# Attention with a top-k search on ScalarE: the counts of each tile's search begin one step later

## What is computed

```python
logits = jnp.einsum('bqhd,bsd->bqhs', iqb, ik)
index = jnp.einsum('bqh,bqhs->bqs', iwb, jax.nn.relu(logits)) * idx_scale
index = jnp.where(causal[None], index.astype(jnp.float32), -jnp.inf)
_, sel = lax.top_k(index, topk)          # topk = 256
kg = jax.vmap(lambda kb, ib: kb[ib])(k, sel)
s = jnp.einsum('bqhd,bqkd->bqhk', qb, kg) * scale
```

## Time and profile before

| | us |
|---|---|
| time before, median of 3 runs (lowest to highest) | 3646.22 (3642.06 to 3647.02) |
| the profiled execution's own time | 3653.36 |
| its span, first to last instruction | 3651.6 |
| PE / DVE / ACT / POOL busy in it | 3431.7 / 2358.1 / 1804.7 / 1210.2 |
| first and last count (L1762) | 507.2 to 1955.0 |

### The profile page before, as it was taken

How to read it: one execution, slowest core, us unless ns; L and a number is a source line. 1 busy time by engine, 2 the same in 40 slices (tenths; PEclk the granted TensorE clock), 3 DMA queues, 4 the chain that set the end, 5 groups by cost and what they waited for, 6 DMA issues and landing times. The chain is left out here.

```text
span 3651.6 us, 55407 instructions
## 1 busy us (share of the span) xinstructions
PE 3431.7 (94%) x18952; PEld 2939.0 (80%) x18952; DVE 2358.1 (65%) x4874; ACT 1804.7 (49%) x3062; POOL 1210.2 (33%) x1966
## 2 busy tenths in 40 slices
PE   6999789899999999999999899799999999999998
PEld 6999767678888878888878688688888788888876
DVE  8999366677776677676674344865554657565354
ACT  3443346677777667867856333433323333333232
POOL 5243244454433333332222033532211425332031
PEclk9999899999999999999999999899999999999999
DMA  4345310000000000000000256232224542332444
GB/s 162 121 152 166 80 32 18 22 20 18 17 14 11 17 10 14 11 8 11 4 7 30 90 161 195 82 115 93 81 93 168 185 133 93 104 102 80 142 141 170
DMA packets 189762, 289.59 MB, mean 79 GB/s; under 512 B 33458, under 2 KB 129842, under 8 KB 189490
## 3 DMA queue, kind: packets, MB, share of 16 engines
q1 hardware_dynamic: 187412, 285.64, 23.8%
q10 hardware_dynamic: 2080, 0.52, 0.1%
HBM read 211.15 MB, written 74.97 MB: 78 GB/s over the span
## 5 line engine op out<-in xcount | busy, mean ns | idle before, releaser
L1755 ACT ACTIVATE shared<-a_ps_st 128x512 f32<-128x512 f32 x716 | 437.6, 615 | 289.8 <-PE a_ps_st L1641 147.4
L2866 PE MATMUL f_ps<-f_x_four,f_w_hi 128*128 128x512 f32 x1408 | 438.2, 393 | 11.4 <-DVE f_w_lo L3004 11.4
L2866 PE MATMUL f_ps<-f_x_three,f_w_hi 128*128 128x512 f32 x1056 | 325.5, 389 | 1.5 <-DVE f_w_lo L3004 1.5
L2866 PEld LDWEIGHTS f_ps<-f_x_four,f_w_hi 128*128 128x128 f32 x1408 | 266.6, 190 | 68.4 <-DVE f_w_lo L3004 13.0
L1665 PEld LDWEIGHTS a_ps_o<-a_vsl,shared 128*128 128x128 f32 x2176 | 297.7, 201 | 19.6 <-DVE a_fin L1972 0.7
L1463 POOL TENSOR_SCALAR a_tk<-a_tk,a_halves 128x1 f32<-128x1 f32 x336 | 108.7, 324 | 588.0 <-ACT a_junk_a L1762 586.3
L1665 PEld LDWEIGHTS a_ps_o<-a_dv,shared 128*128 128x128 f32 x2176 | 285.8, 194 | 12.3
L1665 PE MATMUL a_ps_o<-a_vsl,shared 128*128 128x65 f32 x2176 | 288.9, 278 | 0.0
L1665 PE MATMUL a_ps_o<-a_dv,shared 128*128 128x65 f32 x2176 | 276.7, 271 | 0.0
L2866 PE MATMUL f_ps<-f_x_four,f_w_lo 128*128 128x512 f32 x704 | 275.8, 392 | 0.0
L2899 PE MATMUL f_ps<-f_w_hi 128*128 128x512 f32 x680 | 265.6, 391 | 4.8 <-DVE f_w_lo L3013 4.8
(11 more groups left out here) (382 smaller groups left out, 8794.8 us busy)
## 6 DMA issues: line engine op xcount, KB each, us to landing
shared<-in_w_down SPq DMA_DIRECT2D x88, 512.0 KB, 3.4
px_raw<-in_x_t SPq DMA_DIRECT2D x48, 512.0 KB, 4.7
shared<-in_w_gate SPq DMA_DIRECT2D x44, 512.0 KB, 5.1
shared<-in_w_up SPq DMA_DIRECT2D x44, 512.0 KB, 4.8
g_scratch<-shared SPq DMA_DIRECT2D x22, 1024.0 KB, 7.5
shared<-g_scratch SPq DMA_DIRECT2D x88, 256.0 KB, 3.4
z_scratch<-p_z SPq DMA_DIRECT2D x16, 768.0 KB, 5.2
o_scratch<-a_oacc SPq DMA_DIRECT2D x32, 256.0 KB, 2.1
```

What stands on the lines that cost most here:

```text
L1755: act.activation(p_t[:, s % PT_RING, :], ps_st[s % ST_BANKS][:, :], ACT.Exp, scale=SCALE).then_inc(exp_done, 1)
L2866: mm = pe.matmul(out[:, :], w[:, j, k * P:(k + 1) * P], x_part(j, x)[:, k], start=(k == 0 and i == 0), stop=(k == 3 and i == 2))
```

## The change

One line in `Schedule.set_search`: the first step of the range over which a search's 24 counts are spread is begin + nch + 1 and no longer begin + nch. The last step, the number of counts and everything else of the plan are as they were.

```diff
@@ -833,7 +833,7 @@
                 self.chores[end + 3 + nch + c].append(("pick", t, c))
             self.chores[begin + nch].append(("set", t, 0))
             self.chores[end + 1 + nch].append(("room", t, 0))
-            a, b = begin + nch, end
+            a, b = begin + nch + 1, end
             for m in range(NSTEP):
                 self.counts[a + m * (b - a) // NSTEP].append((t, m))
             begin = end + 1
```

## The result

The change makes the kernel slower by a little: 3651.91 us (median of 17 runs, 3648.68 to 3660.65) against 3646.82 us for the kernel before on the same chips (17 runs, 3642.06 to 3648.86). The ratio is 1.0016, with a 95% interval of 1.0009 to 1.0022: 5 us lost, where 17 were forecast as gained. The profiled execution of the kernel after took 3651.62 us, its span is 3649.8. That is shorter than the span of 3651.6 in which the rows of before stand, though the medians say the opposite. That execution of before was 7 us over its median; a second trace of the kernel before stands further down beside it.

What follows compares the result with a forecast made beforehand. PE, busy 94% of the span, was taken as the bound, so only less idle time or a higher clock could pay. 8.0 + 7.5 - 1.5 - 2 + 5.1 = 17.1 us off 3646.2 gave 3629 us, range 3617 to 3643.

Steps and rivals of the forecast that it cites:

- (a): PE gaps ended by the late exponential at the sets of searches 7, 9, 10, 11, 14: 8.0 us saved.
- (b): PE gaps ended by an ACT copy behind a count, searches 4 to 7: 7.5 us saved.
- (c): Search 8: the first count's threshold move falls behind a POOL addition, so PE loses 1.5 us.
- (d): Other counts meet or leave POOL's waits for DVE's `a_fin`: 2 us lost, bounds 2 gained to 9 lost.
- (e): PE's clock after the gaps of searches 9, 10, 11, 14: 5.1 us gained, bounds 0 and 10.2.
- (f): Searches 2, 3, 12, 13 and 15 costed at nothing; DVE ends PE's stops at the sets of 12, 13, 15.
- The second: Rival: moved counts get behind POOL's additions in searches 2, 5, 8, 9; slower, 3657 us, chance 0.06.
- deciding point: ACT's waiting for POOL grows from 72.2 us by more than PE's saved idle, some 15 us.
- The sign that the prediction set for being wrong: ACT's wait for POOL grows as much as its wait for DVE falls, or PE's gaps stay, ended by DVE.
- The first rival: PE stops at the next bank DVE has not emptied, giving gains back within ten steps; 3642 us, chance 0.19.
- The third: Rival: DVE's set comes later by what ACT comes earlier, so ACT's wait stays; 3646 us, chance 0.02.

Runs made afterwards that it cites:

- two-step kernel: Against the kernel before, counts of searches 4 and 7 begin one step later, those of 9, 10, 11, 14 and 15 two: 3635.66 us, ratio 0.9972.
- All but the first: Count 0 of every search at its old step, the other counts as in the changed kernel; against the kernel before: 3652.91 us, ratio 1.0023.
- first alone: Only count 0 of searches 9 to 15 one step later than in the kernel before: 3644.28 us, ratio 0.9999.
- late alone: The change for searches 9 to 15 only, against the kernel before: 3642.67 us against 3645.02, ratio 0.9997.
- early alone: The change for searches 2 to 8 only, against the kernel before: 3658.04 us, ratio 1.0037.
- 6 alone: The change for search 6 only, against the kernel before: 3656.52 us against 3648.6, ratio 1.0011.

## Why the prediction was wrong

(a) held. The five gaps at the sets went from 1.28, 2.56, 3.07, 3.57 and 2.14 to 0.20, 1.07, 1.60, 2.14 and 0.26 us. That is 7.4 us; 8.0 was the sum. DVE is next, as it said, and the two-step kernel confirms it.

(b) held at most of the gaps it named and failed as a gain. Search 4's 7.05 us became 4.49 (2.6 saved, 2.1 forecast), search 5's gap of 1.15 and search 6's of 1.71 went, search 7's of 1.99 is 0.3; only search 5's second, 1.23, is still 1.06. That is 7.3 us; 7.5 was the sum. But the counts that moved away from these places landed a few steps on. Search 4 gives most of it back at 712.55 (1.51 to 3.21), search 5 at 790.27 (0.68 to 2.18), and search 6 has 1.61 us at 821.30 where it had 1.71 at 815.87. As lengths: search 4 -1.2 us, search 5 +3.1, search 7 -4.9. Search 7's gain is in part luck: the gaps that (a) and (b) named there shrank by 2.8 us, and two that no term named by 2.9 more (2.03 to 0.33 us, and 1.16 to none).

(c) had place and sign right and its size too small: the gap at step a+4 of search 8 grew from 0.90 to 3.18 us, 2.3 for the 1.5 forecast, and the search is 3 us longer. The move behind the addition took 1.7 us (1002.17 to 1003.88) where the sum had 0.7. "All but the first" shows that it is count 0.

(d) is the step that failed. It put the other counts down as "they move rather than vanish", and took -2. It compared counts only with POOL's waits for `a_fin`, and set the waits that went against those that came, as if ACT had slack at the one place as at the other. It left out POOL's other jobs (`prep_q`, `block_mask`), how close counts stand to each other, and which ACT copy, with PE behind it, comes next. ACT's waits for POOL grew by only 4.2 us in sum, but by 13.1 in searches 2 to 8, and in front of each new gap of PE that was followed up stands a count that waited for POOL. The size of the miss can be worked out: (a), (b) and (c) as measured make 7.4 + 7.3 - 2.3 = 12.4 us less idle time, and the gaps of 0.2 us and more fell by 3.3. So everything that none of them names cost 9.1 us of PE's time on balance, where (d) took 2. "All but the first" has these counts moved and the first one where it was (and with them (b)'s gains in searches 4, 6 and 7): it measured a ratio of 1.0023 [1.0014 to 1.0032], 5 to 12 us slower.

(e) failed with it. It took the clock as something to be won only, with bounds of 0 and 10.2. The shorter gaps did give some of it back: none of the 6.8 us at the lower level around search 9's set in the trace of before is left. But in searches 2 to 8 the time lost to the clock rose from 22.2 to 30.7 us, which is their whole loss. Most of it is one gap that is not at a set: it grew from 0.49 to 1.35 us, and the 13.6 us at half clock behind it are 6.8 us lost (in "all but the first" 10.2 us, so 5.1 lost). So the term has a second sign. The Trainium skill, "TensorE: Matmul & The Clock Gate", section "A second HAM failure mode: psum-queue depth-cycling", says that PE idling briefly between groups of matmuls, frequently enough, makes the clock swing, and that the way back up is paid. I had weighed that rule for the gaps that were there. It speaks as much against new ones, and the trace agrees in part: 1.35 us of idle, then 55 matmuls where 99 would have run. But it was one gap that did it here. At that place gaps of 0.83 and 0.49 us cost no clock.

(f) held for searches 2, 3 and 13 within 0.5 us; 15 is 2.8 us shorter, with 3.4 us less lost to the clock. Search 12 didn't hold. The cover I named for it at its set is real (2.25 us, ended by DVE, in the kernel after), but its new gap of 1.90 us is at step 444, 22 steps on, where I hadn't looked.

The rivals. The second, slower by counts that get behind POOL, had the right side and 0.06. It named POOL's additions, and those stand at the gaps of search 8 and two of search 6; at others it is another job of POOL or the move itself. Its deciding point (ACT's wait for POOL up by 15 us) wasn't reached in the stage, 4.2, because the late searches took 8.9 us back; in searches 2 to 8 it was nearly, 13.1. The sign that the prediction set for being wrong, a wait for POOL that grows by as much as the wait for DVE falls, holds there as well (13.1 and 11.6). The first rival, DVE takes ACT's place, is true of each set, and "first alone" shows that the gain can be given back, though more behind ACT's copies than behind DVE. The third is refuted by 65.3 to 40.5 us.

In sum: the early searches lose 8 to 9 us in both traces that move all of them, of them 6.8 at search 6 through the clock; the late ones gain some 2 us in the median of "late alone" (interval -4 to +2).

Open. The parts don't add up to the microsecond: "early alone" is 13 us slower in its median while its stretches hold 9, and what searches 9 to 15 gain or lose varies with stretches of low clock that come and go between executions of one kernel, as search 10 shows. What decides whether a gap is followed by them isn't settled. Moving the first count alone in the early searches was not tried, nor was a kernel in which POOL's `prep_q` gives way to the counts, which would test POOL's part by itself.

## What to carry to other kernels

A list of instructions shifted by one place lands somewhere in every repetition of the pattern. Check each landing place for what stands behind it on its engine, and for what the engine that answers it is doing there (here POOL), not only the place that the shift was made for, and choose repetition by repetition where they don't agree: that was worth 19 us here with the same one-line edit that lost 5 when applied to all. Where TensorE is 94% busy, a stall that the new order creates may cost many times its length through the clock (here 0.9 us more of a gap, then 5.1 to 6.8 us), so a sum of gaps needs a clock term of both signs. A sum of waits over a whole stage can hide this: 4.2 us more was 13.1 more in one half and 8.9 less in the other. And before a single trace is used as the base of a sum, take a second: two traces of one kernel differed by 7 us in two searches, at the same idle time.

## What was unexpected of the hardware

- The growth of one gap from 0.49 or 0.83 us to 1.35 us in search 6 was followed by 13.6 us at 0.50 or 0.51 of full clock in the traces of the kernels "after", "early alone" and "6 alone", and by 10.2 us of it (0.62 over 13.6) in "all but the first". In the nine traces with the smaller gap no low clock follows.
- The same gap of 1.43 us in search 10 was followed by 13.6 us at 0.50 in one execution of the kernel before, and by a clock of 0.87 over the same length in another. The clock is thus no function of the order of work alone. Nor does the length of a gap settle it: behind a new gap of 1.44 us in search 6, 3.4 us at the lower level follow in four traces and none in "6 alone".
- In spite of that, searches 2 to 8 repeat within 0.2 us between two executions, low-clock stretches included.
